# Second-layer value rows as three products of rounded parts, split during the gate sweep

## What is computed

```python
# end of each layer: the sigmoid-gated per-layer input embedding
ple = (p[i] @ w_ple_proj[i]) * jax.nn.sigmoid(h @ w_ple_gate[i])
h = h + rmsnorm(ple, g_ple[i])
...
# layer 1
a = rmsnorm(h, g_mix_pre[i])
z = a @ w_in_c[j]
q_h = z[..., 0:HGRN_WIDTH]
f_h = z[..., HGRN_WIDTH:2 * HGRN_WIDTH]
i_h = z[..., 2 * HGRN_WIDTH:3 * HGRN_WIDTH]
g_h = z[..., 3 * HGRN_WIDTH:4 * HGRN_WIDTH]
qkv = z[..., 4 * HGRN_WIDTH:].reshape(bsz, t, 3, SB_HEADS, SB_HEAD_DIM)
```

## Time and profile before

| | us |
|---|---|
| runs of the kernel before: median of 3 | 1949.39 |
| lowest, highest | 1946.25, 1952.33 |
| the profiled execution, its own time | 1946.59 |
| its span in the trace | 1944.8 |
| PE busy | 1807.3 (93% of the span) |
| DVE busy | 1125.4 (58%) |
| ACT busy | 726.3 (37%) |
| mean granted TensorE clock | 0.959 of full speed |

### The profile page before, as it was taken

The page is one execution under the profiler, slowest core; times in us unless marked ns, Lnnn a source line. Parts: engine busy times, 40 slices in busy tenths (PEclk is TensorE's granted clock), DMA queues, the critical chain, the costliest instruction groups (busy, mean ns, idle before and its releaser), DMA issues.

```text
span 1944.8 us, 34321 instructions
## 1 busy us (share of the span) xinstructions
PE 1807.3 (93%) x13384; PEld 1617.6 (83%) x13384; DVE 1125.4 (58%) x2363; ACT 726.3 (37%) x1313; POOL 38.4 (2%) x65
## 2 busy tenths in 40 slices
PE   6899898989999979999999998887989999979997
PEld 5788456989999979988479995445989999979987
DVE  7974465568777652263334865666568777652264
ACT  5323345543233242254323332656543333242252
POOL 1400000000000000000000000000000000000000
PEclk9999788999999989999999996999999999989999
DMA  4133678212222132221031133773212222132211
GB/s 177 66 61 132 212 260 293 87 42 89 87 79 83 41 132 86 78 90 57 21 108 57 55 124 121 265 266 132 88 44 88 87 80 82 41 132 87 77 44 49
DMA packets 77948, 204.13 MB, mean 105 GB/s; under 512 B 12530, under 2 KB 14882, under 8 KB 77314
## 3 DMA queue, kind: packets, MB, share of 16 engines
q1 hardware_dynamic: 75762, 190.36, 29.3%
q0 software_dynamic: 2064, 12.06, 1.8%
HBM read 190.81 MB, written 10.40 MB: 103 GB/s over the span
## 4 chain that ended last, share of the span: by engine, by line
PE 81%; DVE 9%; SPq 3%; ACT 3%; issue 2%; DMA 1%; DVEq 0%; ACTq 0%
PE psum L412 42%; PE psum L585 12%; PE psum L2203 7%; PE psum L2159 4%; PE psum L420 2%; SPq L1312 2%; PE psum L844 1%; PE psum L2352 1%; PE psum L1354 1%; PE psum L507 1%; PE psum L1329 1%; PE psum L521 1%; DVE sb_arena_r L372 1%; DVE sb_ring_r L372 1%; SPq L1296 1%
## 5 line engine op out<-in xcount | busy, mean ns | idle before, releaser
L412 PE MATMUL psum<-sb_a_sb_r,sb_ring_r 128*128 128x288 f32 x1408 | 297.1, 295 | 0.0
L412 PE MATMUL psum<-sb_a_sb_r,sb_arena_r 128*128 128x288 f32 x1344 | 276.5, 296 | 0.0
L412 PE MATMUL psum<-sb_y_sb_r,sb_ring_r 128*128 128x288 f32 x960 | 262.6, 298 | 0.5 <-DVE sb_ring_r L372 0.5
L412 PEld LDWEIGHTS psum<-sb_a_sb_r,sb_ring_r 128*128 128x128 f32 x1408 | 230.9, 188 | 0.4
L412 PEld LDWEIGHTS psum<-sb_a_sb_r,sb_arena_r 128*128 128x128 f32 x1344 | 217.0, 188 | 0.0
L372 DVE TENSOR_TENSOR sb_ring_r<-sb_ring,sb_ring_r 128x1024 fp32r<-128x1024 f32 (+1 forms) x90 | 116.2, 1295 | 169.1 <-ACT sb_ring_r L369 168.1
L412 PE MATMUL psum<-sb_y_sb_r,sb_arena_r 128*128 128x288 f32 x704 | 207.1, 294 | 6.3 <-DVE sb_a_sb_r L372 6.2
L369 ACT ACTIVATE sb_ring_r<-sb_ring 128x1024 fp32r<-128x1024 f32 (+1 forms) x90 | 99.8, 1114 | 300.6 <-PE psum L412 249.3
L412 PEld LDWEIGHTS psum<-sb_y_sb_r,sb_ring_r 128*128 128x128 f32 x960 | 174.9, 189 | 1.6 <-DVE sb_ring_r L372 1.0
L585 PE MATMUL psum<-sb_arena_r 128*128 128x288 f32 x960 | 161.6, 303 | 8.2 <-DVE sb_arena_r L372 8.2
L412 PE MATMUL psum<-sb_arena_r,sb_ring_r 128*128 128x288 f32 x1056 | 146.0, 299 | 20.9 <-DVE sb_arena_r L372 20.9
(11 more groups left out here) (402 smaller groups left out, 3130.2 us busy)
## 6 DMA issues: line engine op xcount, KB each, us to landing
sb_ring<-w SPq DMA_DIRECT2D x166, 512.0 KB, 3.6
sb_ring<-wd SPq DMA_DIRECT2D x32, 704.0 KB, 4.1
sb_arena<-sb_v SPq DMA_DIRECT2D x64, 256.0 KB, 5.5
sb_arena<-moba_v SPq DMA_DIRECT2D x56, 256.0 KB, 6.4
sb_ring<-moba_k SPq DMA_DIRECT2D x32, 256.0 KB, 4.1
sb_a_sb<-moba_k SPq DMA_DIRECT2D x32, 256.0 KB, 5.6
sb_ring<-sb_k SPq DMA_DIRECT2D x32, 256.0 KB, 4.1
sb_a_sb<-sb_k SPq DMA_DIRECT2D x32, 256.0 KB, 5.5
```

The source lines that it names most:

```text
L412: ins = e.eng.matmul(out[:, half, :], fr(w[p][:, k, :]), fr(x[q][:, k, cols]), start=(first and k == 0 and i == 0), stop=(last and k == kb ...
```

## The change

The value rows of layer 1 are formed from rounded parts: three 128x512 matmuls in place of one unrounded one. The eight row slabs are split by ACT and DVE, the low part over the raw slab in the ring and the high part in the arena (`row_high`). Group 0 is split during the gate sweep (slabs 2 and 3 after A2, slabs 0 and 1 after the squares of half 0), group 1 during r00 and r01. x of half 0 is split behind `dve_pre` in the gate sweep, x of half 1 behind its own `dve_pre`, so that the split of all of x after the last row tile goes. On PE the norm sums of half 1 move into the middle of r00 (before its fifth k-step), and the squares of half 1 from behind r10 to behind r01. Ring slots, loads and the dense tiles stay.

```diff
--- before.py
+++ after.py
@@ -465,6 +465,25 @@
                 e.eng.scalar_tensor_tensor(dst[:, k, :], src[:, k, :], vcol(layer, gain, k), rstd[:, :], ALU.mult, ALU.mult)
 
         COLS = (slice(0, HALF), slice(HALF, T))
+        row_high = [cut(at, 4 * SLAB).rearrange("p (s k n) -> p s k n", s=4, k=KD) for at in (23296, 9216)]
+
+        def act_row_slab(e, g, j, used=None):
+
+            wait_slab(e, 4 * g + j)
+            if used is not None:
+                e.eng.wait_ge(acc_ready, used)
+            act_high(e, slabs[:, 4 * g + j], row_high[g][:, j], wh_ready)
+
+        def dve_row_x(e, k, half):
+
+            e.eng.wait_ge(xh_ready, e.parts + k + 1)
+            dve_low(e, y[:, k, COLS[half]], a[:, k, COLS[half]], y[:, k, COLS[half]], xl_ready)
+
+        def dve_row_slab(e, g, j):
+
+            e.splits += 1
+            e.eng.wait_ge(wh_ready, e.splits)
+            dve_low(e, slabs[:, 4 * g + j], row_high[g][:, j], slabs[:, 4 * g + j], wl_ready)
 
         def sums(at):
 
@@ -2004,17 +2023,25 @@
                     act_slab(e, gate_pairs[4 + 2 * j], 2 * j)
                     act_slab(e, gate_pairs[5 + 2 * j], 2 * j + 1)
                 act_gate_square(e, j, 0)
+                if pre and j == 2:
+                    for n in range(2):
+                        e.fills[n] += 1
+                    for n in (2, 3):
+                        act_row_slab(e, 0, n)
             act_sweep_gate(e, t["B0"], 0, 1)
             act_rstd(e, t["nA"], COLS[0])
             act_gate_square(e, 0, 1)
             if pre:
                 act_squares(e, 0)
+                for n in range(2):
+                    act_row_slab(e, 0, n, t["B1"].n)
             act_sweep_gate(e, t["B1"], 1, 1)
             act_gate_square(e, 1, 1)
             act_sweep_gate(e, t["B2"], 2, 1)
             act_gate_square(e, 2, 1)
             if pre:
                 act_rstd(e, t["pA"], COLS[0])
+                act_split_half(e, y, a, 0, (x_new, 2 * KD * e.pre))
             act_sweep_gate(e, t["B3"], 3, 1)
             act_gate_square(e, 3, 1)
 
@@ -2080,9 +2107,15 @@
             dve_part_sum(e, gate_sums[0], 2)
             e.part_sqs += 4
             e.part_sums += 2
+            if pre:
+                for n in (2, 3):
+                    dve_row_slab(e, 0, n)
             product(3, 0)
             product(0, 1)
             dve_update(e, layer, "g_ple", 0)
+            if pre:
+                for n in range(2):
+                    dve_row_slab(e, 0, n)
             product(1, 1)
             dve_part_sum(e, gate_sums[1], 1)
             product(2, 1)
@@ -2091,7 +2124,13 @@
             e.part_sums += 2
             if pre:
                 dve_pre(e, layer + 1, "g_mix_pre", 0)
+                for k in range(6):
+                    dve_row_x(e, k, 0)
             product(3, 1)
+            if pre:
+                for k in (6, 7):
+                    dve_row_x(e, k, 0)
+                e.parts += KD
 
 
         def sp_layer_end(ld, at, up_stage, pre):
@@ -2148,36 +2187,41 @@
 
         def rows_tiles(acc):
 
-            order = ["r00", "n", "r01", "r10", "p", "r11"] + [f"r{g}{i}" for g in range(2) for i in (2, 3, 4)]
+            order = ["n", "r00", "r01", "p", "r10", "r11"] + [f"r{g}{i}" for g in range(2) for i in (2, 3, 4)]
             return {x: acc.next("act") for x in order}
 
-        def pe_rows(e, t, g, i):
+        def pe_rows(e, t, g, i, ks=range(KD), parts=None):
 
             n = P if i < 4 else NS
-            wait_emptied(e, t)
-            for k in range(KD):
-                last = e.eng.matmul(psum[0:n, 2 * t.s, :], y[:, k, i * P:i * P + n], slabs[:, 4 * g:4 * g + 4, k, :],
-                                    start=(k == 0), stop=(k == KD - 1))
-            last.then_inc(acc_ready, 1)
+            if 0 in ks:
+                wait_emptied(e, t)
+            for k in ks:
+                if parts is not None:
+                    e.eng.wait_ge(xl_ready, parts + k + 1)
+                for z, (x, w) in enumerate(((a, row_high[g]), (a, slabs[:, 4 * g:4 * g + 4]), (y, row_high[g]))):
+                    last = e.eng.matmul(psum[0:n, 2 * t.s, :], fr(x[:, k, i * P:i * P + n]), fr(w[:, :, k, :]),
+                                        start=(k == 0 and z == 0), stop=(k == KD - 1 and z == 2))
+            if KD - 1 in ks:
+                last.then_inc(acc_ready, 1)
 
         def pe_proj_c(e, acc):
             t = rows_tiles(acc)
-            e.eng.wait_ge(x_new, 2 * KD * e.pre + KD)
-            for g in range(2):
-                for i in range(4):
-                    wait_slab(e, 4 * g + i)
-                pe_rows(e, t[f"r{g}0"], g, 0)
-                if g == 0:
-                    pe_late_sums(e, t["n"], gate_sums)
-                else:
-                    wait_emptied(e, t["p"])
-                    pe_squares(e, psum[:, 2 * t["p"].s, 0:HALF], 1, range(KD)).then_inc(acc_ready, 1)
-                pe_rows(e, t[f"r{g}1"], g, 1)
+            e.eng.wait_ge(wl_ready, e.splits + 4)
+            pe_rows(e, t["r00"], 0, 0, range(4), e.parts)
+            pe_late_sums(e, t["n"], gate_sums)
+            pe_rows(e, t["r00"], 0, 0, range(4, KD), e.parts)
+            pe_rows(e, t["r01"], 0, 1)
+            wait_emptied(e, t["p"])
+            pe_squares(e, psum[:, 2 * t["p"].s, 0:HALF], 1, range(KD)).then_inc(acc_ready, 1)
+            e.splits += 8
+            e.eng.wait_ge(wl_ready, e.splits)
+            for i in range(2):
+                pe_rows(e, t[f"r1{i}"], 1, i)
             e.pre += 1
-            e.eng.wait_ge(x_new, 2 * KD * e.pre)
             for g in range(2):
                 for i in (2, 3, 4):
-                    pe_rows(e, t[f"r{g}{i}"], g, i)
+                    pe_rows(e, t[f"r{g}{i}"], g, i, parts=e.parts + KD if g == 0 and i == 2 else None)
+            e.parts += 2 * KD
             for m in range(10):
                 pe_tile_c(e, acc.next("act"), m)
             for m in (10, 11):
@@ -2196,16 +2240,12 @@
             e.eng.wait_ge(wl_ready, e.splits)
             wait_emptied(e, t)
             for k in range(KD):
-                if m == 0:
-                    e.eng.wait_ge(xl_ready, e.parts + 2 * k + 2)
                 for half in range(2):
                     for i, (p, q) in enumerate(((0, 0), (0, 1), (1, 0))):
                         last = e.eng.matmul(pair(t.s)[:, half, :], fr(pair_c(m)[p][:, k, :]),
                                             fr((a, y)[q][:, k, COLS[half]]), start=(k == 0 and i == 0),
                                             stop=(k == KD - 1 and i == 2))
             last.then_inc(acc_ready, 1)
-            if m == 0:
-                e.parts += 2 * KD
 
         def act_slab_c(e, m, used):
 
@@ -2236,16 +2276,19 @@
                 e.eng.activation(d[:, i, :] if i < 4 else ds[0:NS, :], psum[0:n, 2 * t[f"r{g}{i}"].s, :], ACT.Copy)\
                     .then_inc(copied["act"], 1)
 
+            for n in range(2):
+                act_row_slab(e, 1, n)
+            act_rstd(e, t["n"], COLS[1])
+            for n in (2, 3):
+                act_row_slab(e, 1, n)
+            act_squares(e, 1)
             rows(0, 0)
-            act_rstd(e, t["n"], COLS[1])
-            act_squares(e, 1)
             rows(0, 1)
-            act_split_half(e, y, a, 0, (x_new, 2 * KD * e.pre))
-            rows(1, 0)
             act_rstd(e, t["p"], COLS[1])
-            rows(1, 1)
             act_split_half(e, y, a, 1, (x_new, 2 * KD * e.pre + KD))
             e.pre += 1
+            rows(1, 0)
+            rows(1, 1)
             for i in (2, 3, 4):
                 rows(0, i)
 
@@ -2272,8 +2315,15 @@
             v, do = e.eng, e.st.do
             tt = v.tensor_tensor
             rows_tiles(acc)
+            for n in range(2):
+                dve_row_slab(e, 1, n)
             dve_update(e, 0, "g_ple", 1)
+            for n in (2, 3):
+                dve_row_slab(e, 1, n)
             dve_pre(e, 1, "g_mix_pre", 1)
+            for k in range(KD):
+                dve_row_x(e, k, 1)
+            e.parts += KD
             m, e0, e1, lb, oml, t0, t1, t2 = lbt[:8]
             a0, a1 = (vec[:, NVEC + VEC[x]:NVEC + VEC[x] + 4] for x in ("lb0", "lb1"))
             do(tt(m, a0, a1, ALU.max))
@@ -2288,15 +2338,7 @@
             do(tt(lb, e0, e1, ALU.add))
             do(tt(lb, lb, e0, ALU.subtract))
             do(v.tensor_scalar(oml, lb, -1.0, 1.0, ALU.mult, ALU.add))
-            for n in range(2):
-                dve_slab_c(e, n)
-            v.wait_ge(acc_ready, acc.n)
-            for k in range(KD):
-                for half in range(2):
-                    v.wait_ge(xh_ready, e.parts + KD * half + k + 1)
-                    dve_low(e, y[:, k, COLS[half]], a[:, k, COLS[half]], y[:, k, COLS[half]], xl_ready)
-            e.parts += 2 * KD
-            for n in range(2, 4):
+            for n in range(4):
                 dve_slab_c(e, n)
             for m in range(8):
                 dve_slab_c(e, m + 4)
@@ -2317,6 +2359,7 @@
```

(1 more changed line is left out.)

## The result

| | before | changed |
|---|---|---|
| median, us | 1949.02 (4 runs) | 1923.87 (4 runs) |
| lowest, highest | 1946.25, 1952.33 | 1923.57, 1931.93 |
| profiled execution, its span | 1946.59, 1944.8 | 1923.84, 1922.0 |
| mean granted clock | 0.959 | 0.961 |

The account below looks back on a forecast made before the run. PE work was taken to bound the stretch from B3 to the first dense tile: 61.5 us in place of 75.99, 14.5 less 0.1, gain 14.4. From the median 1949.39 this gave 1935.0 us, range 1929.5 to 1941.

Parts of the forecast that it names:

- The rows: Ten row tiles on PE: 240 rounded matmuls at 0.232 us, 55.7 us in place of 69.17, giving 13.5 us.
- the rival at 0.216: Rounded matmuls in the row tiles take 0.216 us each: 3.8 us more, gain 18.2, 1931.2 us; chance 0.12.
- The 0.1 us taken off for two more switches: On PE, two more switches between rounded and unrounded matmuls cost 0.1 us, lowering the gain from 14.5 to 14.4.
- The wait at the dense tiles: PE's wait on DVE's split of x ahead of the first dense tile goes, slabs come in time: gain 1.0 us.
- The covers: PE's work hides added ACT and DVE steps, with 1.1 us at r00, 1.4 at norm sums, 1.4 at r10; cost nothing.
- the rule of the Trainium skill that was weighed: About 1.38 us of drain per ACT table switch; r00 would wait about 1.6 us and the gain be 12.8.
- "After the stretch": From the dense tiles on, all moves up as a block, costed at nothing, 1 us either way for clock pauses.
- The 3 us to either side for the runs' spread: Runs' spread on the whole kernel's time, 3 us to either side, used in setting the range's ends.
- A sign that came up: The prediction is wrong if pieces behind the dense tiles start less than 14 us earlier.
- The slower rival: A stall at r00's head drops the clock; all ten row tiles at half clock would be 41 us slower; chance 0.03.

## Why the prediction was right and wrong

**The rows: right.** Starts in the changed kernel, in two of the three groups of L2202 (min/median/max ns, first and last start):

```profile
L2202 PE MATMUL psum<-sb_arena_r,sb_a_sb_r x80: 389/394/615, 915.3 to 976.1; 128*128 128x512 f32 x64, 128*64 128x512 f32 x16
...
L2202 PE MATMUL psum<-sb_arena_r,sb_y_sb_r x80: 389/397/398, 915.8 to 976.5; 128*128 128x512 f32 x64, 128*64 128x512 f32 x16
```

44.49 / 192 = 0.232 us each. Taking the row of the same instruction over two halves of an unrounded record was right; the rival at 0.216 fell. The 0.1 us taken off for two more switches between rounded and unrounded matmuls had no row behind it and doesn't show: the two pieces behind a switch run at 8.35 / 36 and 44.49 / 192, 0.232 us, like the first, and the 61.5 us held without it.

**The wait at the dense tiles: right.** It went, and the slabs came in time.

**The covers: right.** With 1.1 us taken off for the later start, the steps came where the working put them: `dve_pre` at 909.2 (forecast 909.3), the first low part of x at 912.6, DVE through with the last two slabs at 929.6 (929.9), low parts of half 1 done at 938.8 (938.8). The rows of ACT and DVE:

```profile
910.88 3.45 ACT L369 ACTIVATE sb_a_sb_r<-sb_y_sb 128x288 fp32r<-128x288 f32 x8 [0.59 <-DVE sb_y_sb L580]
914.35 1.28 ACT L1934 ACT_TABLE_LOAD   x1
915.64 0.65 ACT L1934 ACTIVATE sb_a_sb<-psum 128x576 f32<-128x576 f32 x1
```

```profile
910.33 3.52 DVE L580 SCALAR_TENSOR_TENSOR sb_y_sb<-sb_h_sb,sb_vec,sb_rstd 128x288 f32<-128x288 f32 x8 [1.53 <-ACT sb_rstd L513]
913.77 2.30 DVE L372 TENSOR_TENSOR sb_y_sb_r<-sb_y_sb,sb_a_sb_r 128x288 fp32r<-128x288 f32 x6
...
928.41 2.36 DVE L372 TENSOR_TENSOR sb_ring_r<-sb_ring,sb_arena_r 128x1024 fp32r<-128x1024 f32 x2
...
936.92 3.03 DVE L372 TENSOR_TENSOR sb_y_sb_r<-sb_y_sb,sb_a_sb_r 128x288 fp32r<-128x288 f32 x8
```

The table load follows the split by 0.02 us and the sigmoid the table load by 0.01 us: no drain here either, so the rule of the Trainium skill that was weighed (ScalarE: Activation LUTs, section What ACT_TABLE_LOAD costs) doesn't show as time in this chain.

**"After the stretch": wrong, and this is the step that failed.** It said that what follows moves up as a block, "with 1 us either way for pauses that fall differently against the clock". As far as the transposes the block did move up: dense to transposes is 160.7 or 160.8 us in both first traces and stays within 0.3 us of that in all the others. But the term for the clock was 1 us where the first two traces differ by 8.5 in the first part of the recurrence alone (31.8 and 23.3), and all traces together by up to 5.8 over the rest behind it (758.9 to 764.7). It can be seen in the trace before: the window of 0.53 over 21 us of busy PE. I had read the clock for the stretch that was changed and for one stall in the gate sweep, and took only pauses for a risk; the recurrence has PE busy for all of the 21.00 us, almost all of them at half the clock. Had the stretch been priced at both levels, the range would have gone down by 8.5 us, to about 1921, and held the time; that the draw would favour the changed kernel couldn't be read from the trace before. The 3 us to either side for the runs' spread were too small as well: they came from three runs, and 109 reach from 1935.8 to 1956.8.

**A sign that came up.** The prediction called itself wrong if the pieces behind the dense tiles started less than 14 us earlier. Counted from the start of the span they do: the first dense tile starts 13.4 us earlier and the first transpose 13.6 (1137.5 for 1151.1). That is the 1.1 us by which the changed trace is late ahead of the change; counted from the first row matmul it is 14.6.

The slower rival looked for the same mechanism in the wrong place and with the wrong sign: in the rows the clock was 1.00 throughout.

What stays open: what decides whether the clock falls ahead of the last small matmuls or behind them. The 128x8 matmuls and the pause ahead are in both cases; filling the pause changed nothing that the runs can tell. Why the places of the two unmoved kernels are as they are wasn't settled either, and how much of the gap between the medians, beyond the 14.6 us of the stretch, would be left over many places isn't known: 1.5 us by one average, 2.8 by the other, each with some 5 us of uncertainty.

## What to carry to other kernels

When an edit moves a long kernel by a few microseconds, later stretches can be granted another clock, as one with small matmuls was here: look in the trace before for stretches with a granted clock near 0.5 and busy PE, price each at both levels, and put that in the range. Judge such an edit by the stretch it changes, and by both kernels moved by several small amounts; here one place says 22.7 us, another 9.1, their average 15.4 (16.1 with the moved work taken off) and the stretch itself 14.6. Where three rounded matmuls replace one unrounded, the price is that of the rounded one in the same kernel (0.232 against two records of 0.432), and it is had in full only if the splits are ready before PE asks.

## What the runs showed of the hardware

- A rounded 128x512 matmul starts every 0.232 us at full clock (L2202, 240 of them), and an unrounded one takes two records of 0.432 (L2159); three for one save 20%. At half a record, 0.216, each, they would have saved 25%.
- The clock can be at 1.2 GHz for 30.8 us in which PE is busy without a break (1163.2 to 1194.0 in the trace before); up to 1182.9 the work was groups of 128x128 and 128x8 matmuls. It fell in the recurrence in all 20 traces, 12 to 26 us behind the first transpose; over the whole span their mean granted clock is 0.958 to 0.964.
- The kernel before varied from 1935.8 to 1956.8 in 109 runs, 1.1% from end to end, more than the 0.3% that I took for its measurement.
